# Four 32x32 diagonal blocks in place of two 64x64 halves for the first levels of a triangular inverse

## The reference, cut to what matters

```
kb = kc * bc[..., None]
lmat = jnp.where(strict, jnp.einsum('nbhid,nbhjd->nbhij', kb, kc) * decay, 0.0)
rhs = jnp.concatenate([kb * jnp.exp(gc)[..., None], vc * bc[..., None]], axis=-1)
sol = lax.linalg.triangular_solve(eye + lmat, rhs, left_side=True, lower=True, unit_diagonal=True)
...
v_new = u_i - jnp.einsum('bhck,bhkv->bhcv', w_i, S)
o = (q_i * exp(g_i)) @ S + qk_i @ v_new
S = S * exp(g_last) + k_dec^T @ v_new
```

## Time and profile before

| | us |
|---|---|
| median of the runs | 3641.97 |
| the profiled execution | 3635.77 |
| its span | 3634.1 |
| busy in the span: TensorE matmul | 3350.6 |
| VectorE | 2024.5 |
| ScalarE | 756.3 |
| GpSimd | 859.0 |

### The profile page before, as it was taken

How to read it: one execution, slowest core, us unless ns; L and a number is a source line. 1 busy time by engine, 2 the same in 40 slices (tenths; PEclk the granted TensorE clock), 3 DMA queues, 4 the chain that set the end, 5 groups by cost and what they waited for, 6 DMA issues and landing times.

```text
span 3634.1 us, 63994 instructions
## 1 busy us (share of the span) xinstructions
PE 3350.6 (92%) x27323; PEld 3162.3 (87%) x27323; DVE 2024.5 (56%) x4339; ACT 756.3 (21%) x1577; POOL 859.0 (24%) x775
## 2 busy tenths in 40 slices
PE   6989898989998999988999999995599899999998
PEld 4878787979797888878999999994499799999997
DVE  5556666575756666667867767636512433333334
ACT  3323232323232423222000110112200300000001
POOL 2102120202020202112333333322223233333331
PEclk8999999999999999999999999996699899999999
DMA  2111111111111111110122222226611011111111
GB/s 91 55 48 49 54 50 60 41 54 56 51 50 43 60 42 61 48 37 30 49 79 72 79 75 83 77 72 205 178 41 47 24 48 47 49 47 47 48 48 60
DMA packets 111305, 223.12 MB, mean 61 GB/s; under 512 B 24880, under 2 KB 59184, under 8 KB 110000
## 3 DMA queue, kind: packets, MB, share of 16 engines
q1 hardware_dynamic: 82400, 177.66, 15.8%
q10 hardware_dynamic: 28624, 41.38, 3.5%
HBM read 177.86 MB, written 41.14 MB: 60 GB/s over the span
## 4 chain that ended last, share of the span: by engine, by line
PE 86%; DVE 8%; DMA 2%; ACT 2%; issue 1%; SPq 1%; POOL 0%; POOLq 0%; DVEq 0%; ACTq 0%
PE ps L218 31%; PE ps L624 15%; PE ps L1340 14%; PE ps L657 7%; PE ps L704 5%; PE ps L234 1%; PE ps L679 1%; PE ps L692 1%; PE ps L651 1%; PE ps L636 1%; PE ps L295 1%; PE ps L729 1%; PE ps L685 1%; PE ps L673 1%; PE ps L642 1%
## 5 line engine op out<-in xcount | busy, mean ns | idle before, releaser
L218 PE MATMUL ps<-hhi,whi 128*128 128x344 f32 x2424 | 778.7, 321 | 19.3 <-DVE hlo L1809 14.7
L218 PE MATMUL ps<-hhi,wlo 128*128 128x344 f32 x2424 | 776.0, 320 | 0.0
L218 PE MATMUL ps<-hlo,whi 128*128 128x344 f32 x2424 | 775.2, 320 | 0.0
L2078 POOL TENSOR_TENSOR wtick<-wtick 128x1 f32<-128x1 f32 x213 | 59.2, 278 | 2571.4 <-PE ps L218 817.4
L2081 POOL TENSOR_TENSOR wlo<-wraw,whi 128x1024 fp32r<-128x1024 f32 x213 | 531.8, 2497 | 17.1
L218 PEld LDWEIGHTS ps<-hhi,whi 128*128 128x128 f32 x2424 | 457.4, 189 | 22.4 <-issue 16.6
L218 PEld LDWEIGHTS ps<-hhi,wlo 128*128 128x128 f32 x2424 | 457.0, 189 | 0.0
L218 PEld LDWEIGHTS ps<-hlo,whi 128*128 128x128 f32 x2424 | 456.4, 188 | 0.1
L624 PE MATMUL ps<-hhi,whi 128*128 128x344 f32 x1152 | 388.3, 337 | 6.6 <-DVE olo L1056 2.7
L624 PE MATMUL ps<-hhi,wlo 128*128 128x344 f32 x1152 | 371.7, 323 | 0.0
L624 PE MATMUL ps<-hlo,whi 128*128 128x344 f32 x1152 | 371.0, 322 | 0.0
(11 more groups left out here) (358 smaller groups left out, 5385.4 us busy)
## 6 DMA issues: line engine op xcount, KB each, us to landing
wraw<-in_w SPq DMA_DIRECT2D x213, 512.0 KB, 3.6
dwork<-keep_rows SPq DMA_DIRECT2D x64, 256.0 KB, 3.7
tab<-keep_tab SPq DMA_DIRECT2D x8, 1088.0 KB, 6.5
S<-in_sin ACTq DMA_DIRECT2D x16, 512.0 KB, 3.8
drw<-keep_del SPq DMA_DIRECT2D x32, 256.0 KB, 3.3
out_sout<-S ACTq DMA_DIRECT2D x16, 512.0 KB, 2.7
keep_u<-hs SPq DMA_DIRECT2D x8, 580.0 KB, 3.4
uu<-keep_u SPq DMA_DIRECT2D x8, 580.0 KB, 7.9
```

Source lines behind the costliest of these rows:

```text
L218: ins = nc.tensor.matmul(out, w, r[:, kt, blk(n)], start=k == 0, stop=k == 3 * KT - 1)
L2078: G.tensor_tensor(wtick[:, 1:2], wtick[:, 0:1], wtick[:, 0:1], ALU.add)
```

## The change

Levels 1 to 4 now run on the four 32x32 diagonal blocks of each matrix. M's diagonal blocks are put side by side in 32 columns (three copies by ScalarE, `diagonal`, in place of L1094), all four masks are applied by one product of VectorE (NM, 512 elements a partition), and the first T comes from VectorE's 32x32 transpose in place of the product with the identity. T and Y of a quad lie in one buffer TY, so that a level's sums are one operation of VectorE; the set of 16 matmuls of 32x32 goes to four tiles on the diagonal of the array and four banks. Level 5 joins pairs of 32-blocks to 64-blocks by products of just the blocks that are not zero, and only T's upper half (buffer TOP) and Y itself are written out, by small copies of ScalarE (`spread_t`, `spread_y`, `fifth_y`) and one of VectorE. Level 6 is as before, but waits for the Y5 of ScalarE. Y's buffers are set to zero once in the prolog.

```diff
-            def tiles(banks, col, lhsT, rhs):
-                for half, h, c in TILES:
-                    r = slice(H * half, H * half + H)
-                    ins = nc.tensor.matmul(ps[r, banks[h], col + c * H:col + (c + 1) * H], lhsT(r, 2 * h + c), rhs(r, 2 * h + c), start=True, stop=True)
+            def tiles(col, lhsT, rhs):
+                for d in range(4):
+                    for j in range(4):
+                        r = zone((j + d) % 4)
+                        ins = nc.tensor.matmul(ps[r, LEV[j], col:col + Z], lhsT(r, j), rhs(r, j), start=True, stop=True)
                 return ins
...
+            def fifth_level(i, q):
+                slot(i, q, 8)
+                p.after("DVE", gq + "TY4")
+                for j in range(4):
+                    for h in range(2):
+                        jj = (j + h) % 4
+                        up, low = zone(2 * h), zone(2 * h + 1)
+                        ins = nc.tensor.matmul(ps[low, LEV[jj], COL_P:COL_P + Z], DEC[q % 2][up, jj, low], W[up, jj, 0:Z], start=True, stop=True)
+                p.go(ins, gq + "P5")
+                slot(i, q, 9)
+                p.after("ACT", gq + "P5")
+                for j in range(4):
+                    ins = nc.tensor.matmul(ps[zone(1), LEV[j], COL_T:COL_T + Z], W[zone(1), j, Z:2 * Z], PP[zone(1), j], start=True, stop=True)
+                p.go(ins, gq + "T5")
...
+                        ins = nc.tensor.matmul(ps[up, LEV[jj], COL_Y:COL_Y + Z], PP[low, jj], W[low, jj, Z:2 * Z], start=True, stop=True)
+                p.go(ins, gq + "PY5")
...
+                slot(i, q, 10)
                 p.after("DVE", gq + "T5")
+                p.after("ACT", gq + "Y5")
...
             def levels(i, q):
-                for l in range(1, 7):
+                for l in range(1, 5):
                     slot(i, q, 2 * (l - 1))
...
+                    if l == 1:
+                        p.after("DVE", gq + "NM")
+                    p.after("DVE", gq + f"TY{l - 1}")
+                    p.go(tiles(COL_P, lambda r, j: NM[r, l - 1, j], lambda r, j: W[r, j, 0:Z]), gq + f"P{l}")
                     slot(i, q, 2 * (l - 1) + 1)
                     p.after("ACT", gq + f"P{l}")
...
+                    tiles(COL_T, lambda r, j: W[r, j, Z:2 * Z], lambda r, j: PP[r, j])
+                    p.go(tiles(COL_Y, lambda r, j: PP[r, j], lambda r, j: W[r, j, Z:2 * Z]), gq + f"PY{l}")
+                fifth_level(i, q)
+                last_level(i, q)
...
@@ ScalarE @@
+            def diagonal(i, q):
+                a.after("DVE", g + "NT")
+                for z in range(1, 4):
+                    a.go(A.activation(DEC[q % 2][zone(z), :, 0:Z], DEC[q % 2][zone(z), :, zone(z)], AF.Copy), g + "NTc")
+            def spread_t(i, q):
+                a.after("DVE", g + "TY4")
+                for z in range(2):
+                    a.go(A.activation(TOP[zone(z), :, zone(z)], TY[q % 2][zone(z), :, 0:Z], AF.Copy), g + "TOP")
+            def spread_y(i, q):
+                for z in range(4):
+                    a.go(A.activation(YY[q % 2][zone(z), :, zone(z)], TY[q % 2][zone(z), :, Z:2 * Z], AF.Copy), g + "YD")
+            def fifth_y(i, q):
+                a.after("PE", g + "PY5")
+                for z in (0, 2):
+                    a.go(A.activation(YY[q % 2][zone(z), :, zone(z + 1)], across(COL_Y, Z, zone(z)), AF.Copy), g + "Y5")
...
+                if s == 9:
+                    spread_t(i, q)
+                    if q + 1 < NQ:
+                        diagonal(i, q + 1)
+                    spread_y(i, q)
                 if s == 10:
+                    fifth_y(i, q)
                     a.after("PE", g + "vT")
...
@@ VectorE, first_y @@
+                W, M = TY[q % 2], DEC[q % 2]
+                v.after("ACT", g + "NTc")
+                v.go(V.tensor_tensor(W[:, :, Z:2 * Z], M[:, :, 0:Z], lev[:, 0].unsqueeze(1).to_broadcast([P, 4, Z]), ALU.mult), g + "Y0a")
+                v.go(V.tensor_tensor(W[:, :, Z:2 * Z], W[:, :, Z:2 * Z], idz[:, :].unsqueeze(1).to_broadcast([P, 4, Z]), ALU.add), g + "Y0")
+                v.go(V.tensor_tensor(NM, M[:, :, 0:Z].unsqueeze(1).to_broadcast([P, 4, 4, Z]), lev[:, 1:5].unsqueeze(2).to_broadcast([P, 4, 4, Z]), ALU.mult), g + "NM")
+                v.go(V.transpose(W[:, :, 0:Z], W[:, :, Z:2 * Z]), g + "TY0")
@@ VectorE, the levels @@
+                            v.after("PE", gq + f"PY{l}")
+                            v.go(V.tensor_tensor(W, across(COL_T, 2 * Z), W, ALU.add), gq + f"TY{l}")
                         elif l == 5:
+                            v.after("PE", gq + "T5")
+                            v.go(V.tensor_copy(TOP[zone(1), :, 0:Z], across(COL_T, Z, zone(1))), gq + "T5")
```

More of the change, by code:

```diff
@@ L555, in build, with zone, across @@
         SLOTS = 12
-        COL_P, COL_T, COL_Y, COL_T0 = 0, P, 0, P
-        TILES = [(half ^ h, h, c) for half in range(2) for c in range(2) for h in range(2)]
+        COL_P, COL_T, COL_Y = 0, Z, 2 * Z
         DENSE = (0, 1, 2, 3, 5, 6, 7)
[L559 to L565, removed]
+        LEV, CB = (0, 1, 2, 3), 4
+        def zone(a_):
+            return slice(Z * a_, Z * a_ + Z)
+        def across(col, w, r=slice(0, P)):
+            return ps[r, 0:4, col:col + w]
         PIECE_SLOTS = ((0, 1, 2, 3, 4, 7, 8, 9), (0, 2, 3, 4, 6, 7), (0, 3, 4, 7, 8), (0, 3, 4, 6, 7))
@@ L760, in last_level @@
                 Y = YY[q % 2]
+                slot(i, q, 10)
                 p.after("DVE", gq + "T5")
+                p.after("ACT", gq + "Y5")
                 for j in range(4):
-                    ins = nc.tensor.matmul(ps[H:P, LEV_A[0], j * H:(j + 1) * H], DEC[q % 2][0:H, j, H:P], TT_[0:H, j], start=True, stop=True)
+                    ins = nc.tensor.matmul(ps[H:P, LEV[0], j * H:(j + 1) * H], DEC[q % 2][0:H, j, H:P], TOP[0:H, j], start=True, stop=True)
                 p.go(ins, gq + "P6")
@@ L766, in last_level @@
                 p.after("ACT", gq + "P6")
-                p.after("DVE", gq + "Y5")
                 b = aside("DVE", gq + "Y6", (i * NQ + q + 1) * SLOTS)
                 for j in range(4):
-                    ins = nc.tensor.matmul(ps[0:H, b, j * H:(j + 1) * H], PP[H:P, j], Y[H:P, j, H:P], start=True, stop=True)
+                    ins = nc.tensor.matmul(ps[0:H, b, j * H:(j + 1) * H], PP6[H:P, j], Y[H:P, j, H:P], start=True, stop=True)
                 p.go(ins, gq + "PY6")
@@ L818, in mix_pe @@
                     levels(i, q)
[L819 to L822 removed]
+                for b in LEV:
+                    held[b] = ("ACT", f"{i}.{NQ - 1}.P6")
             e = HQK - 1
@@ L1244, in mix_dve @@
                 first_y(i, 0)
-                level_mask(i, 0, 1)
+                v.go(V.memset(TOP[0:Z, :, Z:2 * Z], 0.0))
                 for q in range(NQ):
                     gq = f"{i}.{q}."
-                    Y = YY[q % 2]
+                    Y, W = YY[q % 2], TY[q % 2]
                     for l in range(1, 7):
@@ L2058, in _ @@
             done = 3 * LV - 1
+            for z in range(4):
+                G.tensor_copy(lev[zone(z), :, :], wide[zone(z), :, zone(z)]).then_inc(lev_done, 1)
+                pool.wait_ge(lev_done, done + 1)
+                G.tensor_copy(idz[zone(z), :], ident[zone(z), zone(z)]).then_inc(lev_done, 1)
+                pool.wait_ge(lev_done, done + 2)
+                done += 2
             for half in range(2):
-                r = slice(H * half, H * half + H)
-                G.tensor_copy(lev[r, :, :], wide[r, :, r]).then_inc(lev_done, 1)
+                G.memset(YY[half][:, :, :], 0.0).then_inc(lev_done, 1)
                 pool.wait_ge(lev_done, done + 1)
-                G.tensor_copy(idh[r, :], ident[r, r]).then_inc(lev_done, 1)
-                pool.wait_ge(lev_done, done + 2)
-                G.memset(YY[half][H:P, :, 0:H], 0.0).then_inc(lev_done, 1)
-                pool.wait_ge(lev_done, done + 3)
-                done += 3
+                done += 1
             G.memset(eps_t[:, 3:4], 0.0).then_inc(const_ready, 1)
```

99 lines of the change are left out of this document (30 added, 69 removed).

## The result

The changed kernel is slower: 3665.54 us (median of 7 runs) beside 3640.00 (7 runs of the kernel before on the same chips), ratio 1.0057, 95% interval 1.0039 to 1.0075. (The ratio is that of the means; the quotient of the two medians is 1.0070.) Forecast were 3582 us and a gain. The profiled execution took 3668.19 us, 32 us more than that of before. It is the slowest of the seven, and the profiled one of before is faster than all seven runs beside it, so the traces show a larger difference than the medians (26 us) or the ratio (21 us).

The account below looks back on a forecast made before the run. TensorE was taken to set the pace. Terms -81 (level sets), -20 (fifth level), -30 (first transpose), -8 (masks), +49 (Y5 wait), +20 (joined sums), +10 (clock) gave -60 us: 3582 us, range 3525 to 3670.

Parts of the forecast that it names:

- The level sets: TensorE's sets in levels 1 to 4: 0.256 us each for 0.467, at 8 ns a record, 384 sets, -81 us.
- A: Rival for the level sets: records handed over no faster than 20 ns each, sets +66 us, 3684 us in all; chance 0.12.
- A': Rival for the level sets: a floor of 25 ns on every record, sets +128 us, 3737 us in all; chance 0.03.
- The fifth level: Level 5's matmuls on TensorE: fewer records on the tiles, -0.63 us a quad, -20 us.
- The first transpose: Leaves TensorE: -15 us of matmuls and -15 us of waiting; VectorE's own, 0.2 to 0.68 us, hidden in a wait.
- P6's wait: TensorE waits at the last level for ScalarE's Y5: 6.6 us a head, +53 us, +49 less the old wait.
- The joined sums: One VectorE sum starts only after the whole set, so TensorE may wait: 2.5 us a head, +20 us (0 to +40).
- The masks: VectorE's six mask products a quad become one, ending a late one per head: 1 us a head, -8 us (0 to -14).
- The clock: New waits invite stretches at 1.2 GHz on TensorE: about one more a head that matters, +10 us.
- The window of one head: One head's inverse: 7 to 8 us shorter, TensorE busy some 14 us less, granted clock 0.93 to 0.97.
- sign of a wrong mechanism: In the level sets and one head's inverse: sets don't shorten, or they do and the head's window stays.
- Rival D: Sets of 32-wide tiles leave the clock at 1.2 GHz through the inverse: 3900 us or so; chance 0.04.

Follow-up runs that it names:

- e: Kernel before, 64x64 tiles, with four of eight matmuls left out of each set of levels 1 to 4 (some operands scaled by zero): 3592.4 us, 0.9886 of before.
- i: Kernel before with half of each set of levels 1 to 5 and six of eight matmuls of the first transpose left out: 3596.9 us, 0.9897 of before.
- j: As i, with the last level also waiting for four added ScalarE copies behind the next quad's NT: 3631.0 us, 0.9985 of before.
- c: Changed kernel with the three NTc copies moved to VectorE and T5's copy to ScalarE, a shorter way to Y5: 3646.3 us, 1.0021 of before.
- run b: Changed kernel with every set of 32x32 matmuls of levels 1 to 4 issued twice: 3910.3 us, 1.0740 of before.

## Why the forecast was wrong

**The level sets** were right: 0.45 and 0.76 us for 0.68 and 1.15 are -0.62 us a level, -79 us in all, forecast -81. That it is so near is in part luck: the records come each 9.7 ns and not 8, which is 21 us more, and what a set takes beyond its records fell from 0.21 to 0.14 us, which the forecast had not. Rivals A and A' are out: records come each 9.7 ns, not 20. By that the trace does not agree with the 25 ns that the Trainium skill's page TensorE: Matmul & The Clock Gate, "Back-to-back issue gap", gives, as a limit for records on different tiles.

**The fifth level** was right: P5 0.44 us and the other two sets some 0.6 (965.90 to 966.49 us), 1.03 for 1.83, -26 us for -20. **The first transpose** and its wait are gone, as forecast; VectorE's own took 0.30 us in a gap, in the bounds.

**P6's wait** was right in place and cause, and in size by sums that cancel: 55 us to the stage's end where 53 in all were forecast. By quads it is 0.7, 2.9, 1.6 and 1.7 us where 1.4, 2.9, 1.5 and 0.8 were forecast. In the quad worked the wait is 2.90 us where it said 2.9, but both of its ends are off by 0.45 us: counted from the level-4 sum at 963.83, P6 starts at 6.15 us and not at 5.7 (NTc, YD and Y5 take 0.97, 1.30 and 0.56 us for 0.8, 1.05 and 0.5), and TensorE is done at 3.25 and not at 2.8.

**The joined sums** cost less: L660 waits 8.1 us for sums and 4.6 for copies where L657 waited 2.4 and 7.1 in the same window, some 3 us more for 20. Beside them stand 5.3 us at "issue", which the kernel before has not.

**The masks** were put at -8 us. TensorE's wait for L1124 was 1.5 us in the whole stage before, in one piece, so there was less to gain by that; no run shows the term by itself.

**The clock** is the step that failed: "I count about one more a head that matters, +10 us". It is not one stretch more a head but 35 us more a head at 1.2 GHz, 283 in all, worth 96 to 125 us by the quads' slopes and 73 us by the scatter among executions, where 10 stood in the sum. The forecast took the clock from one fall behind a stall, as a price for each new wait. The change made each set a third shorter and put waits behind them, so the same schedule stood with less in it; runs e, i and j show that less work in the sets, in j with the wait too, raises the low time from 79 to 154, 198 and 256 us without narrow tiles (with the zeros named there as an open rival). The window of one head, forecast at 0.93 to 0.97, is 0.82 in the window of the same length and 0.85 from P1 to PY6. The forecast named as a sign of a wrong mechanism that the sets shorten and the head's window stays. That is what happened: the window grew by 3 us. What it had wrong is that work saved at the full clock is time saved.

**Rival D** (32-wide tiles leave the clock at 1.2 GHz through the inverse) had the right quantity and the wrong reason and size: the clock was 0.82, not 0.5, and of the stage's 128 P sets of 32x32 matmuls 92 ran wholly at the full clock (0.45 us). The sum of the forecast without its clock term, -70 us, lies in the 36 to 88 us that the stage would have gained at the old low time. That is worked out from slopes, not measured by a run; no run held the clock up in the changed kernel.

What is open: what exactly the chip counts; why c has as much low time as the changed kernel with half of the waiting; how much of the low time in e, i and j is owed to zeros; and how much of the last 106 us belongs to the narrow tiles.

## What to carry to other kernels

Matmul time taken out of a stage whose engine then waits can lower its clock, and the rest of the stage pays: here 90 us of work taken out gave back 41, and the lower clock took 20 to 33 of the rest. Before forecasting a gain from shorter matmuls, read the granted clock at the places where the engine is least filled, and price the low stretches that the change invites at a quarter to nearly a half of their length. Then move work that is needed into the new gaps (transposes here), and after that try even useless matmuls. And where a term of a forecast is checked, check its parts: two terms here came out near by errors that cancel.

## What the runs showed of the hardware

- Small records on four tiles start 9.7 ns apart (32 records more in 0.31 us), for loads of 32x32 that last 113 ns and 32 moving columns.
- TensorE seems to run short of instructions: 24,576 records of 32x32 matmuls in this stage in place of 12,288 made it stand 96 us at "issue", in pieces of up to 2.9 us (run b; that instructions come too late is a reading, not tested).
- Matmuls of one line start among those of the line before where they lie on another tile. In the changed kernel T5 (L767) and PY5 (L773) mix:

```profile
966.05 0.22 PE L773 MATMUL ps<-dwork 32*32 32x32 f32 x2
966.08 0.19 PE L767 MATMUL ps<-dwork 32*32 32x32 f32 x1
...
966.10 0.19 PE L773 MATMUL ps<-dwork 32*32 32x32 f32 x1
966.11 0.19 PE L767 MATMUL ps<-dwork 32*32 32x32 f32 x1
```

- Small copies of ScalarE (32 partitions by 128) last 0.30 to 0.31 us each from SBUF and 0.26 to 0.27 from PSUM.
- Among executions of one kernel the low time differs by some 50 us, and a microsecond of it costs 0.26 us.
